# Where the dot products of gathered expert rows stand: 8 a block in the routing phase instead of 16, 56 in the last phase instead of 32

## The reference, cut to what matters

```python
def block(xb):                                   # 128 tokens
    qy = (xb @ w_query).reshape(n_tok, PEER_HEADS, 2, half)
    s1 = jnp.einsum('nhd,hkd->nhk', qy[:, :, 0], sub_keys_1)
    s2 = jnp.einsum('nhd,hkd->nhk', qy[:, :, 1], sub_keys_2)
    v1, i1 = lax.top_k(s1, PEER_TOPK)            # 16 of 128 keys, twice, for each of 8 heads
    v2, i2 = lax.top_k(s2, PEER_TOPK)
    cand = v1[..., :, None] + v2[..., None, :]   # 256 pairs, of them again the best 16
    ...
    gates = jax.nn.softmax(top_s, axis=-1)
    u = expert_u[eidx]                           # 8 * 16 = 128 experts of 16384 for each token
    vv = expert_v[eidx]
    act = jax.nn.gelu(jnp.einsum('nhkd,nd->nhk', u, xb), approximate=False)
    return jnp.einsum('nhk,nhkd->nd', gates * act, vv)
```

## Time and profile before

| | |
|---|---|
| median of three runs | 1940.23 us (1934.69, 1940.23, 1942.44) |
| the profiled execution, time of the launch | 1938.46 us |
| its span, first to last instruction | 1936.7 us |
| PE busy | 1752.8 us, 91% |
| PE weight loads busy | 1575.0 us, 81% |
| DVE busy | 1405.9 us, 73% |
| ACT busy | 696.8 us, 36% |
| POOL busy | 478.2 us, 25% |
| mean granted TensorE clock | 0.932 of full speed |
| moved by DMA | 404.54 MB, 209 GB/s over the span |

### The profile page before, as it was taken

How to read it: one execution, slowest core, us unless ns; L and a number is a source line. 1 busy time by engine, 2 the same in 40 slices (tenths; PEclk the granted TensorE clock), 3 DMA queues, 4 the chain that set the end, 5 groups by cost and what they waited for, 6 DMA issues and landing times. The chain is left out here.

```text
span 1936.7 us, 28859 instructions
## 1 busy us (share of the span) xinstructions
PE 1752.8 (91%) x9881; PEld 1575.0 (81%) x9881; DVE 1405.9 (73%) x2542; ACT 696.8 (36%) x1050; POOL 478.2 (25%) x340
## 2 busy tenths in 40 slices
PE   6997689798698999989859998999699999999997
PEld 3875686443476889989859998998699999999996
DVE  4787742289724248888989998987588888888886
ACT  4662121233523234334224443442233333333333
POOL 1000000000101046767642332235222222222220
PEclk9998896667899999999879999999899999999999
DMA  3220000000112336878667887899899999999993
GB/s 113 97 96 22 1 1 1 35 22 1 44 65 76 141 112 187 280 240 286 214 211 265 317 328 289 297 339 393 292 360 330 362 333 356 343 345 351 340 356 114
DMA packets 149007, 404.54 MB, mean 209 GB/s; under 512 B 14100, under 2 KB 71700, under 8 KB 145464
## 3 DMA queue, kind: packets, MB, share of 16 engines
q1 hardware_dynamic: 108600, 243.99, 37.7%
q0 software_dynamic: 36864, 134.23, 18.3%
q10 hardware_dynamic: 3456, 25.17, 3.2%
HBM read 350.90 MB, written 52.44 MB: 208 GB/s over the span
## 5 line engine op out<-in xcount | busy, mean ns | idle before, releaser
L1547 PE MATMUL bank<-h_hi,rt_u_hi 128*128 128x384 f32 x1024 | 356.4, 348 | 33.5 <-DVE rt_u_lo L1337 23.7
L1679 PE MATMUL bank<-va_w_hi,va_v_hi 128*128 128x384 f32 x1024 | 343.8, 336 | 14.9 <-DVE va_w_lo L1644 14.9
L1549 PE MATMUL bank<-h_hi,rt_u_lo 128*128 128x384 f32 x1024 | 347.4, 339 | 0.0
L1548 PE MATMUL bank<-h_lo,rt_u_hi 128*128 128x384 f32 x1024 | 347.2, 339 | 0.0
L1680 PE MATMUL bank<-va_w_lo,va_v_hi 128*128 128x384 f32 x1024 | 343.5, 335 | 0.0
L1681 PE MATMUL bank<-va_w_hi,va_v_lo 128*128 128x384 f32 x1024 | 343.5, 335 | 0.0
L1265 ACT ACTIVATE rt_u_hi<-raw 128x1024 fp32r<-128x1024 f32 x128 | 135.6, 1060 | 408.7 <-PE bank L1549 408.4
L1630 ACT ACTIVATE va_v_hi<-raw 128x1024 fp32r<-128x1024 f32 x128 | 135.7, 1060 | 344.6 <-PE bank L1681 337.9
L1308 POOL DMA_INDIRECT h<-u_rows_dram,own_experts x128 | 168.5, 1317 | 280.0 <-DVE rt_waste L1344 270.1
L1755 POOL DMA_INDIRECT qy<-v_dram,own_experts x128 | 131.1, 1024 | 407.3 <-DVE va_own L1664 401.3
L1644 DVE TENSOR_TENSOR va_v_lo<-raw,va_v_hi 128x1024 fp32r<-128x1024 f32 x128 | 156.8, 1225 | 102.0 <-ACT va_v_hi L1630 102.0
(11 more groups left out here) (324 smaller groups left out, 2846.2 us busy)
## 6 DMA issues: line engine op xcount, KB each, us to landing
raw<-u_dram SPq DMA_DIRECT2D x128, 512.0 KB, 4.5
raw<-v_dram SPq DMA_DIRECT2D x128, 512.0 KB, 6.3
active_scratch<-rt_act SPq DMA_DIRECT2D x128, 192.0 KB, 5.7
gates_scratch<-early ACTq DMA_DIRECT2D x24, 1024.0 KB, 7.3
early<-gates_scratch SPq DMA_DIRECT2D x16, 1536.0 KB, 12.9
early<-active_scratch SPq DMA_DIRECT2D x128, 192.0 KB, 6.8
in_raw<-w_in_dram SPq DMA_DIRECT2D x22, 512.0 KB, 3.5
query_raw<-w_query_dram SPq DMA_DIRECT2D x16, 512.0 KB, 3.5
```

The source lines that it names most:

```text
L1547: mm(bank, u_hi[:, j % 2, cols], hi[:, c, 0:TD], start=c == 0, stop=False)
L1548: mm(bank, u_hi[:, j % 2, cols], lo[:, c, 0:TD], start=False, stop=False)
L1549: last = mm(bank, u_lo[:, j % 2, cols], hi[:, c, 0:TD], start=False, stop=c == DC - 1)
L1679: mm(bank, v_hi[:, j, cols], w_hi[:, j, :], start=start, stop=False)
```

## The change

It alters three things. `DOTS` and `FIRST_DOT` give the phases 24, 48 and 56 dot products instead of 48, 48 and 32. `best_pairs` no longer has a dot product behind each head, `best_keys` keeps its own. And GpSimd issues a gather only behind the `u_lo` of the first eight tiles of a body (from tile 17 on; the first gather, ahead of the loop, is as before), which are those that `best_keys` takes.

```diff
--- before.py
+++ after.py
@@ -1084,8 +1084,8 @@
     START = (0, 64, 112)
     TOK = 8
     RING = 4
-    DOTS = (16, 16, 32)
-    FIRST_DOT = (0, 48, 96)
+    DOTS = (8, 16, 56)
+    FIRST_DOT = (0, 24, 72)
     ld_u, keys_in = ahead["u"], ahead["keys"]
     kept_a = [t.sem(f"rt_active_stored{i}") for i in range(4)]
     sent = [t.sem(f"rt_chunk_sent{i}") for i in range(2)]
@@ -1316,8 +1316,9 @@
                 gather(0)
                 for e in range(BODY + 1, START[1]):
                     low(e)
-                    gather(e - BODY)
-                for k in range(START[1] - BODY, SLOTS):
+                    if e % BODY < PH:
+                        gather(PH * (e // BODY - 1) + e % BODY)
+                for k in range(FIRST_DOT[1], SLOTS):
                     gather(k)
                 pool.wait_ge(s["placed"], 2 * BODY * BODIES[1])
                 ahead["gather"](range(RING))
@@ -1386,8 +1387,6 @@
                         link(d.match_replace(cwork[:], top[:, h, 0:8], cand[:, h, :], TAKEN))
                         link(d.max(top[:, h, 8:16], cwork[:]))
                         link(d.max_index(pos[:, h, 8:16], top[:, h, 8:16], cwork[:]))
-                        if i:
-                            early_dot(DOTS[0] * (i - 1) + PH + h)
                     d.tensor_tensor(soft[:], top[:], top[:, :, 0:1].to_broadcast([P, PH, PTOP]),
                                     ALU.subtract).then_inc(s["tops"], 1)
 
```

## The result

The changed kernel takes 1949.28 us (median of 20 runs) beside 1939.97 of the kernel before (20 runs): a ratio of 1.0051, 95% interval 1.0038 to 1.0064. It is 9.3 us slower. One of its 20 runs (2283.06 us, granted clock 0.721) fell in a slower state of the chip and is left out of the ratio. The forecast was no measurable change, 1939 us. The time lies in the whole range of 1927 to 1955 and outside the forecast's own, 1932 to 1947, and the interval leaves no doubt that there is a change.

The account below looks back on a forecast made before the run. PE was held up by VectorE's lateness in phase 0 (39.6 us), phase 2 by full DMA engines. On the profiled 1938.46 us, - 36.4 + 38.4 - 1.5 = + 0.5 gave 1939 us, no measurable change; range 1927 to 1955, own range 1932 to 1947.

Parts of the forecast that it names:

- the turn of the ring: Phase 2, four gather buffers: (1.49 + 6.8) / 4 = 2.07 us a step, 51 steps in 105.7 us, 38.4 more than before.
- Phase 0: Tiles up to 65: PE no longer waits for a late VectorE, gaining 36.4 us, bounds 33 and 38.
- does not add up: Phase 0 blocks: VectorE enters each next block about 3 us late, but catches up before PE needs a bank.
- Phase 1: The stage between phases 0 and 2: nothing changes but the numbers of the rows.
- The 1.49: Phase 2: 1.49 us from the start of a dot product to the next gather, part of a buffer's turn.
- The landing of 6.8: Phase 2: a gather lands in 6.8 us, the median over the run, between bounds 6.2 and 7.9.
- The end of the stage: After the last dot product: of 6.3 us until the GELU of all sums, 1.5 gained, bounds 0 and 5.
- The second, the slow ring: Phase 2: landings stay at 7.9 us, costing 52.6 us against 36.4, so 1955 us, slower; chance 0.18.
- The first, the bytes alone: Phase 2: the engines stay full and it grows by 31.9 us, so 1927 us, faster; chance 0.20.
- the cheapest bound: Phase 2: 24 more gathers cost only their bytes, 24 x 0.524 MB at 394 GB/s, 31.9 us.
- The third: Phase 2: PE idles in every tile and its clock falls, 1958 us at most; chance 0.06.
- The fourth: Phase 0: something else ends as late; with half of tile 64's gain lost, 1949 us; chance 0.04.

## Why the prediction was wrong

The mechanisms and their places were right, and one term, the turn of the ring in phase 2, was too small. The prediction also took 0.5% as the least that can be told from no change; the interval of 20 runs is 0.13% to either side, so +0.51% is a change.

**Phase 0, right.** Forecast 36.4 us of gain, measured 34.8, and 34.2 by the kernel that has only this half. Tile 64 was to start near 979 us with a wait of 2 to 5: it started at 983.11, or 979.9 without the 3.2 us by which tile 0 was late, and waited 1.55 us for VectorE, a little less than said. (The text has VectorE 3 us late there, the sum took 3.2.) Block 2 was to start near 834: 838.70, so 835.5. That lateness "does not add up" held here, but the kernels that put dot products back show how little room there was: 6 us at block 2 became 11 at block 3.

**Phase 1, right:** 272.0 us against 271.8.

**Phase 2, wrong in size.** The failed step is "(1.49 + 6.8) / 4 = 2.07 us a step, 105.7 us". The 1.49 measured 1.5. The landing of 6.8 measured 7.4 on average (median 7.2): it fell less from the 7.9 of phase 2 before than the lighter load had promised. And a term is missing from the sum: 0.3 us pass from a landing to the dot product, since VectorE takes its work in order and a row may land while it is busy. The turn is 9.2 us, 9.2 / 4 is 2.3 us, and the 51 steps took 116.5 us, 10.8 more than forecast. About 7 us of that are the landing and 4 the missing term. My two bounds of the landing, 6.2 and 7.9 us, did hold the measured one; the error was to pick 6.8, a median over the whole run, and to forecast "no change" when a landing only 0.6 us longer makes it a change.

**The end of the stage, underrated:** from the last gather to the value stage 5.0 us less in place of 1.5, since the two earlier GELUs are done when the last dot product comes (the last of them starts at 1379.71, the dot product at 1382.50). The 6.3 us ahead of the last GELU went whole; behind it 2.2 us were lost again (6.5 to the value stage in place of 4.3). So phase 2 with its end cost 44.2 us where 36.9 were forecast; with 1.6 missed in phase 0 and 0.2 in phase 1 that is the 9.1 us between the sum of 0.5 and the stage's 9.6.

**The rivals.** The second, the slow ring, is nearest to what happened: the step of 2.28 us is past its threshold of 2.2, though its reason, landings that stay at 7.9, is not what the landings of 7.4 show. Its 1955 took a step of 2.35 and left the end of the stage out. The first, the bytes alone, seems to be what happens with seven buffers: from 32 to 56 dot products the time behind tile 112 grows from 83.1 to 114.5 us, 31.4, where the cheapest bound was 31.9. That closeness is luck in part: from the first gather to the last it grew by 36.7 us (55.7 to 92.4), and the end of the stage gave 5.3 back. The third was right in its sign, the granted clock fell to 0.82, between its two levels, and wrong in its effect: VectorE waited only 0.5 us for ScalarE, so PE's pace did not set the steps. With five buffers it was 0.83 and with seven 0.91, where before had 1.00; the steps went by the ring in all. By the rule of the Trainium skill weighed there ("TensorE: Matmul & The Clock Gate", "Part 1: The HAM clock gate") the clock falls in every step whose transfers outlast its matmuls. The trace agrees in part: 0.82 over 80 us is a fall, but not one for all of the time. The fourth did not come.

**What I read wrongly in the profile:** a DMA share of 1.02 as "full". With three, four, five and seven gathers in flight the share is 0.81, 0.94, 0.99 and 1.03 in the same window, and the rate 278, 337, 374 and 412 GB/s. From 0.94 to 1.03 there was 22% of rate left. The limit of 358 GB/s in the Trainium skill ("DMA: Bandwidth & Descriptors", "Where 436 GB/s comes from"), which the prediction set aside for the trace's 394, is passed by the 412 as well. In the kernel before, the reading did little harm: at 394 GB/s no more than 5% was left to the 412, and seven buffers gave the old split 2.2 us.

**Open:** why the landing grows with the depth, what fills the 3.6 us from a gather's start to its first packet when only three are in flight, and why the kernel with phase 0's half alone took 91.4 us behind tile 112 for the same 32 dot products as before with 85.3; its profiled execution was 5 us over its own median.

## What to carry to other kernels

Moving work from a phase where its engine is late to one where the engine has room costs what the resource that comes with the work can't carry there. Here the same move gives +0.5% with four buffers. With seven it is about even: 32.7 us come back until tile 65 (330.5 to 297.8) and 31.4 go behind tile 112, and 0.9957 and 0.9951 can't be told from the old split's 0.9974. For a ring, count the whole turn (from the issue to the landing under the load of that phase, the wait for an engine that works in order, and the release) and divide by the buffers; and judge the transfers by their rate against the best that a window of the trace shows, not by their busy share. When a step is set by the turn, buy a buffer before moving work.

## What the runs showed of the hardware

One core's transfers, mostly gathers of 4 KB rows, reached 412 GB/s over 60 us with seven gathers in flight; the rate rose by 11% from four to five (337 to 374) and by another 10% with seven. An elementwise operation of VectorE on bf16 (128 x 2048) took 1.23 us where it started ahead of a subtraction of GpSimd, and 3.30 where it started during one. With three or four in flight a gather of 512 KB needs 3.6 to 4.1 us until its first packet and another 2.6 to 3.2 until it has landed; with seven it needs 6.8 and 4.3.
